# Down product of a decoder layer's feed-forward network: its weight blocks, from the fourth on, are requested on ScalarE's DMA queue instead of SyncE's

## The chip, the cores and the metric

The kernel runs on one core of one Trainium2 chip. The metric is the device time of one execution in microseconds (us), taken as the median of several runs. All tensors are float32. TensorE works on pairs: every operand is split into a high part of reduced precision (`fp32r`) and a low part (the rest), and each product is made of three matmuls (high x high, high x low, low x high).

## What is computed

One layer of a hybrid decoder on 1024 tokens of width 1024: feed-forward network 1, a token mixer (RWKV-7 and mLSTM side by side), attention over 256 memory tokens, feed-forward network 2, and a last RMSNorm. The change touches the two feed-forward networks alone:

```python
def _swiglu(h, w_gate, w_up, w_down):
    return (jax.nn.silu(h @ w_gate) * (h @ w_up)) @ w_down

x = x + 1/2 * SwiGLU_1(RMSNorm(x))      # D_MODEL = 1024, D_FF = 2816
...
x = x + 1/2 * SwiGLU_2(RMSNorm(x))
out = RMSNorm(x)
```

## The kernel before

There is no scheduler: each engine has its own instruction stream, written out by hand, and the streams meet at semaphores. Each engine works through its stream strictly in order, and so does each issuer of DMAs. SyncE (SP) issues nearly all loads. ScalarE (ACT) computes and issues a few DMAs of its own.

The function `ffn` exists once per engine and is called for network 1 and network 2. First come the gate and up products. Their result, the activation, has 22 tiles of 128 hidden channels x 1024 tokens, each with a high and a low part, 1 MB in all. Tiles 0 to 19 are stored to DRAM (`a_d`, L671), and the last two stay in SBUF (`act_new`). Then comes the down product, `G[n] += w_down[t].T @ a[t]`, and this is where the change is.

The down product runs in 2 x 22 blocks. The outer loop `h` takes the left and then the right half of the output channels (512 each), and the inner loop `j` takes the 22 hidden tiles in the order of the table `DOWN[h]`; `b = h * 22 + j` numbers the blocks 0 to 43. Block `b` needs

- its weights, 128 x 512 (256 KB), which travel through three steps: `load_down(b)` brings them from `in_wd` into one of three raw buffers `wd_raw[b % 3]` (named `sum_temp` in the trace); ACT rounds them to `v_hi` (`down_hi(b)`, L1630); POOL subtracts and makes `v_lo` (L923). `v_hi` and `v_lo` have four slots;
- its activation tile, brought by `load_tile` into `atile` (six places, L686) or `hhi`/`hlo` (L688, L689).

PE then makes 24 matmuls of 128 x 512 for the block (L1052 to L1054): 4 output groups x 2 halves of the tokens x 3. Of the last four blocks of each half (`TAIL`) the matmuls are ordered by output group, so that the results come out one after the other.

The waits around the change are these. `load_down(b)` waits until POOL has finished block `b - 3`, since the raw buffer is then free (semaphore `f_lo`). `down_hi(b)` waits for the landing of the weights (`f_wd`) and until PE has finished block `b - 4` (`f_prod`). PE waits for POOL's part of block `b` (`f_lo`) and for the tile (`f_load`).

Everything that SP loads for the down product stands in one stream (L703 to L744): weights 0 to 2 with tiles 0 to 5; tiles 6 to 9 (eight DMAs of 512 KB); weights 3; tiles 10 to 12 (six DMAs); four rows of x for the residual sum (`load_x`, L692, 512 KB each); weights 4, 5 and 6; tile 13; weights 7; tile 14; and so on, each later tile waiting until PE has left the place that it goes to. The two long runs of tiles and x in it are called bursts here.

Of the kernel before, what the change touches and what calls it, by code (L numbers as in the profile page):

```python
# [19 lines left out]
HALF = 512  # L20
# [3 lines left out]
FFC = FF // P  # L24
PAIRS = FFC // 2
BLOCKS = 2 * (PAIRS - 1)
TAIL = 4
DOWN = ((0, 1, 2, 3, 4, 5, 20, 21, 6, 7, 8, 9, 10, 11, 12, 13, 14, 15, 16, 17, 18, 19),
        (20, 21, 13, 14, 15, 16, 17, 18, 7, 8, 9, 10, 11, 12, 19, 6, 0, 1, 2, 3, 4, 5))
KIND = (0, 1, 3, 4, 2, 5, 6)  # L30
PLACE = tuple(KIND.index(n) for n in range(7))
WD_SLOTS, WD_RAWS = (3, 0, 1, 2), 3
# [26 lines left out]
ACT = mybir.ActivationFunctionType  # L59
# [36 lines left out]
def product_no(q, n):  # L96
    return 2 + 7 * q + n + 1


def down_no(h, j):  # L100
    return 2 + 7 * BLOCKS + h * (FFC - 1) + j + 1


def lo_no(q, n):
    return 4 + 7 * q + n + 1
# [6 lines left out]
def place_of(h, t):  # L112

    if t >= 20:
        return None
    if t == 19:
        return 6
    if t >= 13:
        return t - 13
    return 7 if h and t == 6 else t  # L120
# [55 lines left out]
def layer_kernel(nc, a, out):  # L176
# [3 lines left out]
    def sem(name):  # L180
        if name not in sems:
            sems[name] = ctx.enter_context(nc.semaphore(name))
        return sems[name]
# [74 lines left out]
    wd_raw = [s2_t, s1_t, s4_t]  # L258
# [121 lines left out]
    def weight_blocks(q):  # L380

        if q % 2 == 0:
            return [raw[:, r, s * HALF:(s + 1) * HALF] for r in range(2) for s in range(2)]
        return [xT[:, 2 * r + s, HALF:T] for r in range(2) for s in range(2)]

    def raw_at(f, q):

        return f_raw[q % 2].at(f, (q // 2 + (1 if q % 2 else 2)) * 32)

    def slot(hi, n):  # L390

        w, v = (whi, v_hi) if hi else (wlo, v_lo)
        return w[:, n // 2, n % 2 * HALF:(n % 2 + 1) * HALF] if n < 4 else v[:, n - 4, :]
# [33 lines left out]
    f_lo = Count2(sem("f_lo"), 4 + 7 * BLOCKS + 2 * FFC)  # L427
# [17 lines left out]
    f_wd = [Count2(sem(f"f_wd{n}"), (2 * FFC - n + WD_RAWS - 1) // WD_RAWS * 16) for n in range(WD_RAWS)]  # L445
# [136 lines left out]
    def _(sp):  # L582
# [72 lines left out]
        def ffn(f, after):  # L655

            wg, wu, wd = (a[f"{n}{f + 1}"] for n in ("wg", "wu", "wd"))
            x_from = x_park if f else a["x"]

            def load_pair(q):  # L660
                p = (q + 2) // 2
                for r in range(2):
                    if q % 2 == 0:
                        sp.dma_start(raw[:, r, :], wg[2 * p + r]).then_inc(f_raw[0].sem, 16)
                    else:
                        sp.dma_start(xT[:, 2 * r:2 * r + 2, HALF:T],
                                     wu[2 * p + r].rearrange("p (s c) -> p s c", s=2)).then_inc(f_raw[1].sem, 16)

            def store_pair(p):
                sp.wait_ge(*f_alo.at(f, 2 * p + 2))  # L670
                sp.dma_start(a_d[p], act_new[:].bitcast(F32)).then_inc(f_store.sem, 16)  # L671

            def load_down(b):
                h, j = divmod(b, FFC)
                if b < WD_RAWS:
                    sp.wait_ge(*f_lo.at(f, lo_no(BLOCKS - 1, PLACE[(1, 4, 6)[b]])))
                else:
                    sp.wait_ge(*f_lo.at(f, lo_no(BLOCKS, b - WD_RAWS)))
                sp.dma_start(wd_raw[b % WD_RAWS][:], wd[DOWN[h][j]][:, h * HALF:(h + 1) * HALF]).then_inc(
                    f_wd[b % WD_RAWS].sem, 16)  # L680

            def load_tile(h, t):
                at = place_of(h, t)
                src, s = a_d[t // 2][:, t % 2], f_load[at // 2].sem
                if at < 6:
                    sp.dma_start(atile[:, at].bitcast(F32), src).then_inc(s, 16)  # L686
                else:
                    sp.dma_start(hhi[:, at - 6, :].bitcast(F32), src[:, 0]).then_inc(s, 16)  # L688
                    sp.dma_start(hlo[:, at - 6, :].bitcast(F32), src[:, 1]).then_inc(s, 16)  # L689

            def load_x(k):
                sp.dma_start(xT[:, k, :], x_from[:, k, :]).then_inc(xc_in[k], 16)  # L692

            sp.wait_ge(split_made, after + credit)
            for r in range(2):
                sp.dma_start(raw[:, r, :], wu[r]).then_inc(f_raw[0].sem, 16)
            sp.wait_ge(*f_lo.at(f, 4))
            load_pair(0)
            sp.wait_ge(*f_tlo.at(f, 2))
            load_pair(1)  # L700
            for q in range(2, BLOCKS):
                sp.wait_ge(*f_lo.at(f, lo_no(q - 2, 5)))
                load_pair(q)  # L703
                if q % 2 == 0:
                    store_pair(q // 2 - 1)
            store_pair(PAIRS - 2)
            last = BLOCKS - 1
            load_down(0)
            sp.wait_ge(*f_store.at(f, (PAIRS - 1) * 16))
            for n, t in ((1, 0), (3, 2), (4, 4)):  # L710
                sp.wait_ge(*f_prod.at(f, product_no(last, PLACE[n])))
                load_tile(0, t)
                load_tile(0, t + 1)
                if t < 4:
                    load_down(t // 2 + 1)
            sp.wait_ge(*f_prod.at(f, product_no(last, 5)))
            for t in range(6, 10):
                load_tile(0, t)
            load_down(3)
            sp.wait_ge(*f_prod.at(f, product_no(last, 6)))  # L720
            for t in range(10, 13):
                load_tile(0, t)
            sp.wait_ge(*f_alo.at(f, 2 * PAIRS))
            for k in range(RC):
                load_x(k)
            for b in range(4, 2 * FFC):
                load_down(b)
                h, j = divmod(b - 6, FFC)
                if b < 6:
                    continue  # L730
                t = DOWN[h][j]
                if h == 0 and t < 7:
                    sp.wait_ge(*f_prod.at(f, down_no(0, j)))
                    load_tile(0, t + 13)
                if h == 1 and t == 21:
                    sp.wait_ge(*f_prod.at(f, down_no(1, j)))
                    for k in range(RC, KD):
                        load_x(k)
                if h == 1 and 13 <= t < 19:
                    sp.wait_ge(*f_prod.at(f, down_no(1, j)))  # L740
                    load_tile(1, t - 13)
                if h == 1 and t == 7:
                    sp.wait_ge(*f_prod.at(f, down_no(1, j)))
                    load_tile(1, 6)  # L744
# [786 lines left out]
    def _(act):  # L1531
# [68 lines left out]

        def ffn(f, gain, hi):

            silu = ACT.Silu

            def take_hi(q, n):

                a11, a12, a21, a22 = weight_blocks(q)
                kind = KIND[n]
                src = (a11, s2_t[:], a12, s3_t[:], s1_t[:], a22, s4_t[:])[kind]
                if kind in (0, 2, 5):  # L1610
                    act.wait_ge(*raw_at(f, q))
                else:
                    act.wait_ge(*f_sum.at(f, 4 * q + {1: 3, 3: 2, 4: 1, 6: 4}[kind]))
                if q:
                    act.wait_ge(*f_prod.at(f, product_no(q - 1, n)))
                elif n < 4:
                    act.wait_ge(unit_used, c.unit + 2 + credit)
                else:
                    act.wait_ge(*f_prod.at(f, 2 if n == 6 else 1))
                activation(slot(True, n), src, ACT.Copy).then_inc(f_hi.sem, 1)  # L1620

            def down_hi(b):
                act.wait_ge(*f_wd[b % WD_RAWS].at(f, (b // WD_RAWS + 1) * 16))
                if b >= 4:
                    act.wait_ge(*down_free(f, b - 4))
                elif b:
                    act.wait_ge(*f_prod.at(f, product_no(BLOCKS - 1, b + 3)))
                else:
                    act.wait_ge(*f_prod.at(f, 2))
                activation(v_hi[:, WD_SLOTS[b % 4], :], wd_raw[b % WD_RAWS][:], ACT.Copy).then_inc(f_hi.sem, 1)  # L1630
# [55 lines left out]
            def chunk_hi(k):  # L1686
                if gain:
                    activation(hi[:, k, :], xT[:, k, :], ACT.Copy, scale=v1(gain, k)).then_inc(*nh_act.sig(f"c{k % 2}"))

            for b in range(3, 2 * FFC):  # L1690
                down_hi(b)
                if b == FFC - 1:
                    square(0)
                    square(1)
                if b == FFC + 1:
                    square(2)
                if b == FFC + 3:
                    square(3)
# [1015 lines left out]
```

## Time and profile before

| | |
|---|---|
| time, median of 3 runs | 2914.01 us (2911.01 to 2915.51) |
| the profiled execution's own time | 2909.36 us |
| its span, first to last instruction | 2907.6 us |
| granted TensorE clock, mean over the span | 0.979 of full |
| PE busy | 2755.8 us (95%) |
| ACT busy | 814.3 us (28%) |
| POOL busy | 1513.3 us (52%) |
| DVE busy | 1349.6 us (46%) |
| moved by DMA | 383.06 MB, mean 132 GB/s |
| down products, first and last PE instruction | about 455 to 700 us, and 2623 to 2870 us of the span |

"Busy" counts compute instructions. An instruction that issues a DMA is listed under the engine's queue (SPq, ACTq) and has its own duration. The DMA queue of SP is q1 in the profile, that of ACT is q10. The chain of waits is followed back from the last instruction; what stands in it is what set the end.

### The profile page before, as it was taken

To read this page: it belongs to the slowest core of one execution; us is meant where nothing else is said; L and a number is where in the kernel's file an instruction comes from. 1 tells how busy PE (TensorE), PEld (TensorE's weight loads), DVE (VectorE), ACT (ScalarE), POOL (GpSimd) and SP (SyncE) were. 2 spreads that over 40 slices of the span, in tenths; PEclk is the share of its full clock that TensorE was granted. 3 is DMA by queue.
4 is the path that set the end of the run, shared out by engine and by line. 5 is a ranking of instruction groups with operands and counts; after the bars stand their busy time and mean duration, and the time that the engine had idled before them with its cause. 6 is when DMAs were issued, how large, how long until landed. Compare 5 with 4: busy or idle time off the path is not lost.

```text
span 2907.6 us, 35919 instructions
## 1 busy us (share of the span) xinstructions
PE 2755.8 (95%) x14214; PEld 2278.1 (78%) x14214; DVE 1349.6 (46%) x1357; ACT 814.3 (28%) x1203; POOL 1513.3 (52%) x899
## 2 busy tenths in 40 slices
PE   6999998999999999998999999998899999998996
PEld 5888887888788877777777778888787888887885
DVE  8444441014456535776777645443346444440203
ACT  4333331112001113443444332213413333331111
POOL 4988882123794623555555434431036988872220
PEclk9999999999999999998999999999999999999998
DMA  3333228252862654344334264113021332338151
GB/s 118 117 116 116 108 99 347 69 202 79 342 222 90 217 192 134 99 106 139 105 103 102 70 226 154 44 58 130 0 87 67 121 113 105 116 120 327 59 181 65
DMA packets 143171, 383.06 MB, mean 132 GB/s; under 512 B 10156, under 2 KB 61612, under 8 KB 128832
## 3 DMA queue, kind: packets, MB, share of 16 engines
q1 hardware_dynamic: 119936, 317.75, 31.7%
q10 hardware_dynamic: 23104, 63.47, 5.8%
q8 instruction: 94, 1.54, 0.2%
q14 instruction: 37, 0.30, 0.0%
HBM read 272.57 MB, written 108.58 MB: 131 GB/s over the span
## 4 chain that ended last, share of the span: by engine, by line
PE 73%; issue 9%; POOL 6%; DVE 5%; DMA 2%; ACT 1%; SPq 1%; ACTq 1%; POOLq 0%; DVEq 0%
PE G L1052 14%; PE G L1054 14%; PE G L1053 14%; PE G L977 8%; PE G L979 8%; PE G L978 8%; PE G L1190 2%; POOL AL L868 2%; PE G L1475 1%; DMA sum_temp<-in_wd 1%; PE G L1227 1%; DMA zrw_d<-po 1%; DVE nt_b L2051 1%; POOL Tr L862 1%; ACTq L1546 0%
## 5 line engine op out<-in xcount | busy, mean ns | idle before, releaser
L939 POOL TENSOR_TENSOR whi<-raw,zero 128x1024 fp32r<-128x1024 f32 x67 | 130.2, 1943 | 472.7 <-PE G L979 387.7
L923 POOL TENSOR_TENSOR v_lo<-sum_temp,v_hi 128x512 fp32r<-128x512 f32 x88 | 117.2, 1335 | 383.6 <-ACT v_hi L1630 383.6
L1052 PE MATMUL G<-hhi,v_hi 128*128 128x512 f32 x800 | 312.0, 390 | 0.0
L1054 PE MATMUL G<-hhi,v_lo 128*128 128x512 f32 x800 | 311.2, 389 | 0.0
L1053 PE MATMUL G<-hlo,v_hi 128*128 128x512 f32 x800 | 311.2, 389 | 0.0
L977 PE MATMUL G<-hhi,whi 128*128 128x512 f32 x688 | 272.3, 396 | 28.8 <-POOL wlo L942 21.9
L978 PE MATMUL G<-hlo,whi 128*128 128x512 f32 x688 | 270.8, 394 | 0.0
L979 PE MATMUL G<-hhi,wlo 128*128 128x512 f32 x688 | 270.3, 393 | 0.0
L1190 PE MATMUL G<-hq,gw 128*128 128x512 f32 x768 | 223.7, 424 | 9.8 <-DVE ev L2330 4.6
L1052 PE MATMUL G<-t_hi,whi 128*128 128x512 f32 x480 | 186.7, 389 | 0.0
L1053 PE MATMUL G<-t_lo,whi 128*128 128x512 f32 x480 | 186.7, 389 | 0.0
L1054 PE MATMUL G<-t_hi,wlo 128*128 128x512 f32 x480 | 186.7, 389 | 0.0
L942 POOL TENSOR_TENSOR wlo<-raw,whi 128x1024 fp32r<-128x1024 f32 x67 | 176.3, 2631 | 5.3
L1190 PEld LDWEIGHTS G<-hq,gw 128*128 128x128 f32 x768 | 139.3, 194 | 48.3 <-issue 20.3
L977 PEld LDWEIGHTS G<-hhi,whi 128*128 128x128 f32 x688 | 130.9, 190 | 58.3 <-POOL wlo L942 22.7
L2237 DVE SCALAR_TENSOR_TENSOR rtmp<-G,nrx 128x1024 f32<-128x1024 f32 x16 | 19.6, 1223 | 335.5 <-PE G L1054 335.4
L1053 PEld LDWEIGHTS G<-hlo,v_hi 128*128 128x128 f32 x800 | 150.2, 188 | 31.7 <-issue 0.5
L1052 PEld LDWEIGHTS G<-hhi,v_hi 128*128 128x128 f32 x800 | 150.2, 188 | 31.5 <-issue 0.5
L1054 PEld LDWEIGHTS G<-hhi,v_lo 128*128 128x128 f32 x800 | 150.2, 188 | 31.2
L1052 PE MATMUL G<-atile,v_hi 128*128 128x512 f32 x384 | 153.8, 400 | 18.2 <-POOL v_lo L923 18.2
L1630 ACT ACTIVATE v_hi<-sum_temp 128x512 fp32r<-128x512 f32 x88 | 55.7, 633 | 399.5 <-PE G L1054 309.2
L919 POOL TENSOR_TENSOR wlo<-sum_temp,whi 128x512 fp32r<-128x512 f32 x120 | 165.3, 1399 | 3.4 <-ACT whi L1620 3.4
(409 smaller groups left out, 6378.9 us busy)
## 6 DMA issues: line engine op xcount, KB each, us to landing
a_d<-act_new SPq DMA_DIRECT2D x20, 2048.0 KB, 6.3
atile<-a_d SPq DMA_DIRECT2D x36, 1024.0 KB, 7.1
gw<-gw_d SPq DMA_DIRECT2D x32, 1024.0 KB, 5.4
raw<-in_wg SPq DMA_DIRECT2D x44, 512.0 KB, 4.0
sum_temp<-in_wd SPq DMA_DIRECT2D x88, 256.0 KB, 3.4
xT<-in_wu SPq DMA_DIRECT2D x40, 512.0 KB, 4.6
gw_d<-gw SPq DMA_DIRECT2D x16, 1024.0 KB, 4.8
hhi<-a_d SPq DMA_DIRECT2D x18, 512.0 KB, 13.2
```

The costliest lines, as they stand in the source:

```text
L868: tt(AL[:, n % 2], Am[:], copies(C_LEV + n * P), ALU.mult).then_inc(*F.sig(f"am{n}"))
L919: tt(slot(False, n), src, slot(True, n).bitcast(F32), ALU.subtract).then_inc(f_lo.sem, 1)
L923: tt(v_lo[:, k, :], wd_raw[b % WD_RAWS][:], v_hi[:, k, :].bitcast(F32), ALU.subtract).then_inc(f_lo.sem, 1)
L939: nc.gpsimd.tensor_tensor(whi[:, k, 0:w], raw[:, k, 0:w], zero[:].to_broadcast([P, w]), ALU.add).then_inc(hi_made, 1)
L942: nc.gpsimd.tensor_tensor(wlo[:, k, 0:w], raw[:, k, 0:w], whi[:, k, 0:w].bitcast(F32), ALU.subtract).then_inc(split_made, 1)
L977: nc.tensor.matmul(dst, wh, hi, start=start, stop=False)
L978: nc.tensor.matmul(dst, wh, lo, start=False, stop=False)
L979: return nc.tensor.matmul(dst, wl, hi, start=False, stop=stop)
L1052: nc.tensor.matmul(dst, wh, hi, start=start, stop=False, skip_group_check=True)
L1053: nc.tensor.matmul(dst, wh, lo, start=False, stop=False, skip_group_check=True)
L1054: return nc.tensor.matmul(dst, wl, hi, start=False, stop=stop, skip_group_check=True)
L1190: last = nc.tensor.matmul(G[3][:, 1, :], gw[:, k, way == 2, t * P:(t + 1) * P], hq[:, t + (way == 1) * KD, :], start=at == 0, stop=at == 3 ...
```

## The change

The weights of blocks 0 to 2 are still issued by SP. Those of blocks 3 to 43 are issued by ACT: 3 and 4 after ACT's last work on the activation, and `load_down(b + 2)` ahead of `down_hi(b)` from then on, so 5 ahead of 3, 6 ahead of 4. The condition of each issue is the same semaphore at the same value as before. It is ACT that waits for it now. On SP the same calls are gone, and the tile and x loads keep their order and their own waits.

```diff
@@ sync: ffn @@
             def load_down(b):
                 h, j = divmod(b, FFC)
-                if b < WD_RAWS:
-                    sp.wait_ge(*f_lo.at(f, lo_no(BLOCKS - 1, PLACE[(1, 4, 6)[b]])))
-                else:
-                    sp.wait_ge(*f_lo.at(f, lo_no(BLOCKS, b - WD_RAWS)))
+                sp.wait_ge(*f_lo.at(f, lo_no(BLOCKS - 1, PLACE[(1, 4, 6)[b]])))
...
             for t in range(6, 10):
                 load_tile(0, t)
-            load_down(3)
             sp.wait_ge(*f_prod.at(f, product_no(last, 6)))
             for t in range(10, 13):
                 load_tile(0, t)
             sp.wait_ge(*f_alo.at(f, 2 * PAIRS))
             for k in range(RC):
                 load_x(k)
-            for b in range(4, 2 * FFC):
-                load_down(b)
+            for b in range(6, 2 * FFC):
                 h, j = divmod(b - 6, FFC)
-                if b < 6:
-                    continue
@@ scalar: ffn @@
+            def load_down(b):
+                h, j = divmod(b, FFC)
+                act.wait_ge(*f_lo.at(f, lo_no(BLOCKS, b - WD_RAWS)))
+                act.dma_start(wd_raw[b % WD_RAWS][:], wd[DOWN[h][j]][:, h * HALF:(h + 1) * HALF]).then_inc(
+                    f_wd[b % WD_RAWS].sem, 16)
...
+            load_down(3)
+            load_down(4)
             for b in range(3, 2 * FFC):
+                if b + 2 < 2 * FFC:
+                    load_down(b + 2)
                 down_hi(b)
```

The order on SP at the end of the second burst, network 1, before (`hhi`, `hlo` and `atile` are activation tiles, `sum_temp` the weights' raw buffers, `xT` the rows of x):

```order
L688 DMA hhi<-a_d 128x1024
L689 DMA hlo<-a_d 128x1024
L679 DMA sum_temp_72<-in_wd 128x512 [waits f_lo]
L688 DMA hhi<-a_d 128x1024 [waits f_prod]
...
L692 DMA xT<-in_x 128x1024 [waits f_alo]
L692 DMA xT<-in_x 128x1024 x3
L679 DMA sum_temp_71<-in_wd 128x512 [waits f_lo]
L679 DMA sum_temp_74<-in_wd 128x512 [waits f_lo]
L679 DMA sum_temp_72<-in_wd 128x512 [waits f_lo]
L686 DMA atile<-a_d 128x2048 [waits f_prod]
L679 DMA sum_temp_71<-in_wd 128x512 [waits f_lo]
L686 DMA atile<-a_d 128x2048 [waits f_prod]
```

and the same place now:

```order
L686 DMA hlo<-a_d 128x1024
L685 DMA hhi<-a_d 128x1024 [waits f_prod]
...
L689 DMA xT<-in_x 128x1024 [waits f_alo]
L689 DMA xT<-in_x 128x1024 x3
L683 DMA atile<-a_d 128x2048 [waits f_prod] x6
```

The weights that stood between tile 9 and tile 10, and behind the x rows, have left SP.

The order on ACT at the start of the down product, network 1, before (`v_hi` are the rounded weights, `act_new` the last two activation tiles):

```order
L1630 ACTIVATE v_hi<-sum_temp_74 128x512 [waits f_prod,f_wd2]
L1644 ACTIVATE act_new<-gs 128x1024 [waits f_gs,f_store]
L1644 ACTIVATE act_new<-gs 128x1024 [waits f_gs]
L1630 ACTIVATE v_hi<-sum_temp_72 128x512 [waits f_prod,f_wd0]
L1630 ACTIVATE v_hi<-sum_temp_71 128x512 [waits f_prod,f_wd1]
```

and now:

```order
L1629 ACTIVATE v_hi<-sum_temp_74 128x512 [waits f_prod,f_wd2]
L1643 ACTIVATE act_new<-gs 128x1024 [waits f_gs,f_store]
L1643 ACTIVATE act_new<-gs 128x1024 [waits f_gs]
L1618 DMA sum_temp_72<-in_wd 128x512 [waits f_lo]
L1618 DMA sum_temp_71<-in_wd 128x512 [waits f_lo]
L1618 DMA sum_temp_74<-in_wd 128x512 [waits f_lo]
L1629 ACTIVATE v_hi<-sum_temp_72 128x512 [waits f_prod,f_wd0]
L1618 DMA sum_temp_72<-in_wd 128x512 [waits f_lo]
L1629 ACTIVATE v_hi<-sum_temp_71 128x512 [waits f_prod,f_wd1]
```

Three weight requests stand together ahead of the rounding of block 3, and then one stands ahead of each rounding, with its own wait for POOL.

## Rows read from the trace of the kernel before

**Rows 1.** The page: the chain of waits, shares of the span by line.

```profile
PE G L1052 14%; PE G L1054 14%; PE G L1053 14%; PE G L977 8%; PE G L979 8%; PE G L978 8%; PE G L1190 2%; POOL AL L868 2%; PE G L1475 1%; DMA sum_temp<-in_wd 1%; PE G L1227 1%; DMA zrw_d<-po 1%; DVE nt_b L2051 1%; POOL Tr L862 1%; ACTq L1546 0%
```

**Rows 2.** The chain in order of time: start us, us, what.

```profile
471.71 14.53 DMA sum_temp<-in_wd
486.98 1.27 POOL v_lo L923
...
2640.32 14.81 DMA sum_temp<-in_wd
```

**Rows 3.** Timeline of PE, network 1, around blocks 3 and 4: start, duration, instruction.

```profile
471.12 0.39 PE L1054 MATMUL G<-atile,v_lo 128*128 128x512 f32 x1
474.83 0.50 PE L1052 MATMUL G<-atile,v_hi 128*128 128x512 f32 x1 [3.32 <-POOL v_lo L923]
...
488.29 0.79 PE L1052 MATMUL G<-atile,v_hi 128*128 128x512 f32 x1 [6.12 <-POOL v_lo L923]
...
495.74 0.39 PE L1052 MATMUL G<-atile,v_hi 128*128 128x512 f32 x1
```

**Rows 4.** The same in network 2.

```profile
2639.49 0.39 PE L1054 MATMUL G<-atile,v_lo 128*128 128x512 f32 x1
2643.71 0.80 PE L1052 MATMUL G<-atile,v_hi 128*128 128x512 f32 x1 [3.83 <-POOL v_lo L923]
...
2657.18 0.80 PE L1052 MATMUL G<-atile,v_hi 128*128 128x512 f32 x1 [4.97 <-POOL v_lo L923]
...
2665.56 0.39 PE L1052 MATMUL G<-atile,v_hi 128*128 128x512 f32 x1
```

**Rows 5.** PE by stretch: us, PE busy (count), granted clock, DMA share, GB/s.

```profile
2643.00:2649.00 6.00, 5.29 (x13) 0.50 1.02 408
```

**Rows 6.** Timeline of SP's queue, network 1, second burst.

```profile
456.54 2.25 SPq L679 DMA_DIRECT2D sum_temp<-in_wd  x1
...
466.60 5.07 SPq L692 DMA_DIRECT2D xT<-in_x  x4
471.71 3.42 SPq L679 DMA_DIRECT2D sum_temp<-in_wd  x3
```

**Rows 7.** Timeline of ACT in both networks; in brackets its idle time and the releaser.

```profile
457.45 2.00 ACT L1644 ACTIVATE act_new<-gs 128x1024 fp32r<-128x1024 f32 x2
...
486.27 1.96 ACT L1630 ACTIVATE v_hi<-sum_temp 128x512 fp32r<-128x512 f32 x3 [12.83 <-DMA sum_temp<-in_wd]
...
501.44 0.63 ACT L1630 ACTIVATE v_hi<-sum_temp 128x512 fp32r<-128x512 f32 x1 [4.81 <-PE G L1054]
...
2626.30 1.99 ACT L1644 ACTIVATE act_new<-gs 128x1024 fp32r<-128x1024 f32 x2
```

**Rows 8.** DMAs issued at 456.5, 773 and 753 us: KB, us to landing; q1 at 773.

```profile
sum_temp<-in_wd SPq DMA_DIRECT2D x1, 256.0 KB, 16.2
...
q1 hardware_dynamic: 55, 0.41, 107.0%
...
zrw_d<-po ACTq DMA_DIRECT2D x1, 512.0 KB, 6.8
...
graw<-in_gates_in SPq DMA_DIRECT2D x1, 512.0 KB, 13.4
```

**Rows 9.** DMA queues from 735 to 738 us: packets, MB, share of 16 engines.

```profile
q1 hardware_dynamic: 220, 0.78, 64.2%
q10 hardware_dynamic: 219, 0.45, 38.8%
```

**Rows 10.** ACT's DMA issues by line: duration ns min/median/max, first and last start.

```profile
L1712 ACTq DMA_DIRECT2D zrw_d<-po x14: 337/338/1019, 749.7 to 880.7; - x14
L1546 ACTq DMA_DIRECT2D h_d<-hlo x2: 609/5090/9570, 723.7 to 727.9; - x2
```

**Rows 11.** Timeline of ACT between the halves of the product, network 1.

```profile
584.40 0.63 ACT L1630 ACTIVATE v_hi<-sum_temp 128x512 fp32r<-128x512 f32 x1 [2.90 <-PE G L1054]
...
593.92 0.63 ACT L1630 ACTIVATE v_hi<-sum_temp 128x512 fp32r<-128x512 f32 x1 [1.26 <-PE G L1054]
```

More of the change, by code:

```diff
@@ L1601, in ffn @@
         def ffn(f, gain, hi):
-            silu = ACT.Silu
+            silu, wd = ACT.Silu, a[f"wd{f + 1}"]
             def take_hi(q, n):
```

## The prediction, made before the changed kernel ran

> **What bounds the kernel now.** I read the page first. The chain of waits is mostly PE's lines, but one line in it is not work: the transfer of the down weights, `sum_temp<-in_wd`, has 1% of the span [rows 1]. The chain in order of time says where: two pieces, one in each network, of 14.5 and 14.8 us, each followed by POOL's `v_lo` of 1.27 us [rows 2]. So twice in the run a 256 KB load is what everything waits for.
>
> PE's timeline at these places shows what it costs. In network 1 PE starts the last matmul of block 2 at 471.12, stands 3.32 us before block 3 and 6.12 us before block 4, and starts block 5 at 495.74 [rows 3]. In network 2 it stands 3.83 and 4.97 us [rows 4]. Behind each pause the granted clock is 0.50, the lower of the two levels (1.2 GHz), for some us [rows 5], so a pause costs more than its length.
>
> The reason for the late weights is on SP's queue. Weights 3 are issued at 456.54 behind eight tile DMAs; weights 4, 5 and 6 at 471.71, only after six more tile DMAs and the four x rows [rows 6]. The DMA engines are full in these stretches (share 1.02, about 410 GB/s [rows 5]), so a request lands when all that stands ahead of it on its queue has gone through: weights 3 took 16.2 us [rows 8]. ACT stood 12.83 us for weights 4 [rows 7], and POOL and PE behind it.
>
> **What the pauses are worth.** In steady state ACT's rounding comes every 4.81 + 0.63 = 5.44 us, released by PE [rows 7]; that is one block of 24 matmuls, 0.2267 us each. From the last matmul of block 2 to the first of block 5 there are 49 starts, 11.11 us at that pace. Network 1 took 495.74 - 471.12 = 24.62 us, so it loses 13.51. Network 2 took 2665.56 - 2639.49 = 26.07 us and loses 14.96. The sum is **28.5 us**. The pauses are 18.2 of it, and the lower clock behind the four pauses is the other 10.2, so 2.6 us for a pause.
>
> **Part 1: weights 3, 4 and 5 leave SP's queue.** ACT is free for its first request when the last `act_new` is done, at 457.45 + 2.00 = 459.45 in network 1 and at 2628.29 in network 2 [rows 7]. It is 3 us later than SP's old request for weights 3, and 12 us earlier than for weights 4. The semaphore for weights 3 and 4 (blocks 0 and 1 done by POOL) has long been reached. When do they land? No load of before was issued by ACT with SP's backlog ahead of it at this depth. The nearest row is ACT's store at 773 us: 512 KB, issued while q1 had the engines (share 1.07), landed after 6.8 us [rows 8]. The other end is the mirror case, SP's load of 512 KB at 753 us, across ACT's backlog and behind two loads of its own queue: 13.4 us [rows 8]. Sooner than 6.8 changes nothing. I take 6.8, since it is the same queue against the same backlog, and my load has half the bytes.
>
> The two queues share the engines packet by packet: from 735 to 738 us, with both full, they had 220 and 219 packets [rows 9]. The bytes differ since the packets do; q10 got 0.45 of 1.23 MB there with the small ones, some 150 GB/s, so each further weight of 0.26 MB lands about 1.8 us after the one before.
>
> From the start of rounding to PE is 2.0 us (486.27 to 488.29 [rows 7, 3]). Network 1: 459.45 + 6.8 + 2.0 = 468.3, and PE wants block 3 at 471.12 + 0.23 = 471.35, so 3.0 us to spare. Network 2: 2628.29 + 6.8 + 2.0 = 2637.1 against 2639.72, so 2.6 us to spare. Weights 4 land at about 468.1 and weights 5 at 469.9; PE wants them at 476.8 and 482.2. All four pauses go: **-28.5 us**. With 13.4 in place of 6.8 block 3 is late by 3.5 and 4.0 us in the two networks; with 2.6 of lower clock each this gives back 12.7, and 15.8 remain.
>
> The Trainium skill, *DMA: Bandwidth & Descriptors*, section "Issuing engines are not separate DMA queues", speaks against the change: DMAs of all issuers end on the same 16 engines, and issuing from several engines only saves the sequencer's time. Taken alone it would leave the weights behind the backlog; the rival below has that in numbers. The packet counts of rows 9 do not agree with it for the latency of one request. The same page, under "Arbitration", has each DMA engine alternate between its queues, which is what the rows show.
>
> **Part 2: SP without the weights.** SP's stream is shorter by 41 requests in each network. Tiles and x keep their conditions. Their queue carries the same bytes minus 0.77 MB in the burst, which now go on the other queue. What is late next? Tiles 6 to 12, issued by 466.6, are first wanted in block 8, some 27 us after block 3 starts; tile 13, issued at 475.1 behind the x rows and weights 4 to 6 [rows 6], in block 15. At the 16.2 us of a full queue they land by 483 and 492, against 498 and 537. Nothing: 0 us.
>
> **Part 3: ACT's new waits.** Each rounding now stands behind a request, and each request behind POOL's finish of block b - 1. In steady state: rounding 0.63, handover and POOL 1.4, request 0.34 [rows 2, 7, 10], 2.4 us in a period of 5.44. The wait for PE ends last, as before. Price 0, as long as a request takes below 3.0 us. While three requests stand together (459.5 to about 461) nothing behind them is ready to round.
>
> Between the halves ACT also squares finished rows, and the request for block 24 waits behind two of these. At 584.40 it rounds block 22, and PE has finished that block at 593.9 [rows 11]. Now block 23 is rounded after POOL's block 22, at about 586.8, and is ready at 588.8, 5.1 us before PE wants it at 593.9. Price 0.
>
> **Sum.** Profiled execution: 2909.4 - 28.5 = 2880.9 us. The median of the runs shown is 4.65 us above the profiled one, so I take the median: 2914.0 - 28.5 = **2885.5 us**, 1.0% faster. What follows each product (norm, stores, next product) waits for its result, so the first network's gain is handed on.
>
> **Rivals.**
> 1. *Weights land late but alone* (the 13.4 us end): pauses before block 3 stay, those before block 4 go. 2914.0 - 15.8 = 2898.2. For it: requests across a full queue did take 7 to 13 us. Against: the slow ones were on the other queue and larger.
> 2. *No overtaking*: ACT's requests wait out SP's backlog, 16.2 us as weights 3 did. Ready at 477.7 and 2646.5, 6.3 and 6.8 us late, plus 5.2 of lower clock: 28.5 - 18.3 = 10.2 gained, 2903.8. This is the rule quoted above. Against it: rows 9, and the 6.8 us of rows 8.
> 3. *No change*: the burst is bound by bytes, the weights take their share from the tiles, and PE waits for tiles instead. 2914. Against it: the 15 us and more to spare in part 2.
> 4. *Slower*: ACT is held in its own requests. One request of ACT took 9.57 us at 727.9 us [rows 10]. If each did so as long as the burst fills the engines, from 459.5 until the tile issued at 475.1 has landed 16.2 us later, 32 us, a block would take 9.57 + 2.1 = 11.7 in place of 5.44: 2.7 blocks instead of 5.9, 17 us lost in each network, and three pauses more in each with 2.6 us of lower clock: 2914.0 - 28.5 + 34 + 15.6 = 2935. It decides from 3.3 us a request. Against it: that row is the last of four large stores in a row on ACT's own queue, which here holds three weights of 256 KB; the 14 stores of 512 KB took 0.34 us in the median and 1.02 at most.
>
> **How the numbers follow.** Forecast 0.78; rival 1 0.08; rival 2 0.06; rival 3 0.04; rival 4 0.04. About 0.2% (6 us) is what a measurement can tell from no change. The first three cases are faster by more: 0.92; same 0.04; slower 0.04. The range goes from 2885.5 less the runs' own spread of 4.5 us, 2881, to rival 1 with 1 us more, 2899; rivals 2 to 4, 0.14 together, lie outside.
>
> **What would show it.** In the changed profile the pauses of PE before blocks 3 and 4 are gone and the granted clock stays at 1.00 there; `sum_temp<-in_wd` is gone from the chain; the weights on ACTq land in some 7 us in the bursts; ACT's requests last 0.34 us; the rounding of block 3 starts at about 466 us and that of block 4 waits for POOL. If PE still stands before block 3, rivals 1 or 2 hold, by the landing time; if it stands before tiles, rival 3; if requests on ACTq exceed 3 us, rival 4.

## The result, and the profile after

| | before | after |
|---|---|---|
| median | 2913.34 us (4 runs) | 2883.69 us (4 runs, 2876.65 to 2883.99) |
| ratio to before, 95% interval | | 0.9894 [0.9879, 0.9909] |
| the profiled execution's own time | 2909.36 us | 2876.65 us |
| its span | 2907.6 us | 2874.9 us |
| granted clock, mean | 0.979 | 0.986 |

The time fell by 1.06%, 30 us, where 28.5 us were forecast. The changed kernel ran twice more as a control, with ratios of 0.9890 [0.9870, 0.9911] and 0.9893 [0.9878, 0.9909].

The chain of waits by line, on the page of the changed kernel, has no weight transfer any more (before: [rows 1]):

```profile
PE G L1045 15%; PE G L1047 15%; PE G L1046 15%; PE G L970 8%; PE G L971 8%; PE G L972 8%; POOL AL L861 2%; PE G L1183 2%; PE G L1468 1%; DMA zrw_d<-po 1%; PE G L1220 1%; POOL Tr L855 1%; DVE nt_b L2054 1%; ACTq L1539 0%; ACT sx L1969 0%
```

PE by stretch (length, busy time and count, granted clock, DMA share, GB/s), where it stood before [rows 3 to 5]; first network 1, then network 2:

```profile
471.00:475.00 4.00, 4.00 (x19) 1.00 1.03 401
...
482.00:488.00 6.00, 6.00 (x28) 1.00 1.03 406
...
2600.00:2660.00 60.00, 60.00 (x266) 1.00 1.02 407
```

PE is busy all the time at full clock, while the DMA engines are as full as before. The bytes are the same, only their order on the engines is not.

ACT's timeline in network 1, the counterpart of [rows 7]:

```profile
456.91 0.86 ACTq L1618 DMA_DIRECT2D sum_temp<-in_wd  x2
457.33 2.00 ACT L1643 ACTIVATE act_new<-gs 128x1024 fp32r<-128x1024 f32 x2
458.83 0.33 ACTq L1618 DMA_DIRECT2D sum_temp<-in_wd  x1
463.88 0.63 ACT L1629 ACTIVATE v_hi<-sum_temp 128x512 fp32r<-128x512 f32 x1 [4.55 <-DMA sum_temp<-in_wd]
...
466.63 0.63 ACT L1629 ACTIVATE v_hi<-sum_temp 128x512 fp32r<-128x512 f32 x1 [2.12 <-PE G L1047]
...
469.10 0.63 ACT L1629 ACTIVATE v_hi<-sum_temp 128x512 fp32r<-128x512 f32 x1 [1.83 <-POOL v_lo L916]
```

Block 3 is rounded at 463.88, 7.0 us after the request, and PE goes over to it only at about 471; block 4 is rounded at 466.63 instead of 486.27. The DMA queues from 463 to 466 us show how the weights got past the backlog (packets, MB, share of 16 engines):

```profile
q1 hardware_dynamic: 228, 0.82, 68.0%
q10 hardware_dynamic: 223, 0.42, 36.3%
```

Both queues moved nearly the same number of packets, as in [rows 9]: the engines take from each in turn. The requests of the burst (KB, median us to landing), SP's tiles issued from 472.5 to 488.2 us first:

```profile
atile<-a_d SPq DMA_DIRECT2D x6, 1024.0 KB, 20.8
```

and ACT's two requests at 456.91:

```profile
sum_temp<-in_wd ACTq DMA_DIRECT2D x2, 256.0 KB, 7.7
```

The two weights take 7.7 us in the median, the first of them, weights 3, 6.9 us, instead of 16.2 [rows 8]. What they gain, the tiles pay. A tile requested at 456.43 us lands after

```profile
hhi<-a_d SPq DMA_DIRECT2D x1, 512.0 KB, 20.4
```

where one requested at 456.04 us took 16.1 us before. The 20.8 us above are no measure of that: five of the six tiles were requested only at 488.64 us and later before, behind weights on the same queue. The first of the six is landed at 493.5 us now (472.69 + 20.8) and was at 490.1 before (475.17 + 14.9), so tiles come 3 to 4 us later. They have that time to spare.

**Where the time went.** Four events, the same in both kernels, mark the ends of three stretches. The first rounding of the down weights starts at 441.30 before and 441.20 after in network 1, at 2609.68 and 2592.16 in network 2; the second of the last four outputs of network 1's down product is taken over by DVE at 701.95 and 688.34; the last step of the program starts at 2894.11 and 2861.42:

```profile
701.95 1.22 DVE L2237 SCALAR_TENSOR_TENSOR rtmp<-G,nrx 128x1024 f32<-128x1024 f32 x1
```

before, and after:

```profile
688.34 1.23 DVE L2240 SCALAR_TENSOR_TENSOR rtmp<-G,nrx 128x1024 f32<-128x1024 f32 x1
```

So the down product of network 1 is 13.5 us shorter (13.61 less the 0.10 at its start), what lies between the networks' products 3.9 us, and the rest with network 2's product 15.2 us. The forecast had 13.51 and 14.96 for the two products. The two control profiles of the changed kernel repeat the products to 0.2 us: 247.14 and 247.13 us in network 1 (247.14 here, 260.65 before), 269.22 and 269.37 from the second event to the end (269.26 here, 284.43 before). The stretch between the products does not repeat: it is 1907.7 us before, and 1903.8, 1912.1 and 1910.8 us in the three profiles of the changed kernel. So its 3.9 us can't be put down to the change.

One part of them can be seen. In the profile of before, a spell of lower clock lies at 1698 us, at the end of the token mixer, and the changed kernel's profile has none there. PE by stretch before, and the same place after, 16 us earlier in the program's time:

```profile
1698.00:1705.00 7.00, 6.46 (x18) 0.56 0.94 360
```

```profile
1682.00:1689.00 7.00, 4.21 (x18) 1.00 1.00 385
```

By DVE's steps, the changed kernel is 14.1 us ahead in front of this place (`Bm<-cst,G` at 1617.59 and 1603.47) and 15.8 us behind it (`mo<-sg,G` at 1717.57 and 1701.81). So 1.6 us go with the spell. Another 1.7 us come near 2015 us (`mx<-G` at 2018.93 and 2001.41), where the clock was 0.83 before (2010 to 2020 us) and 1.00 after (1994 to 2004 us).

Such spells come and go between executions of one kernel: the control run has one at 1645 us (`1645.00:1655.00`: clock 0.52) that neither of these two has, and by DVE's steps it is 4.2 us behind the first profile in front of it (`Bm<-cst,G` at 1607.67 against 1603.47) and over 8 us behind at its end. Its span is 2884.1 us, not 2874.9.

### The profile page after: what moved, and what is told of

Same layout as the page of the kernel before. It is cut to its first block, busy times and chain, and to the rows that moved or that the text cites. A ratio compares the mean times of both kernels' runs of the same rounds, so it can differ in the third digit from the quotient of the medians.

```text
span 2874.9 us, 35919 instructions
## 1 busy us (share of the span) xinstructions
PE 2739.7 (95%) x14214; PEld 2267.4 (79%) x14214; DVE 1349.6 (47%) x1357; ACT 812.7 (28%) x1203; POOL 1512.2 (53%) x899
## 4 chain that ended last, share of the span: by engine, by line
PE 74%; issue 10%; POOL 7%; DVE 4%; DMA 2%; ACT 1%; ACTq 1%; SPq 0%; POOLq 0%; DVEq 0%
PE G L1045 15%; PE G L1047 15%; PE G L1046 15%; PE G L970 8%; PE G L971 8%; PE G L972 8%; POOL AL L861 2%; PE G L1183 2%; PE G L1468 1%; DMA zrw_d<-po 1%; PE G L1220 1%; POOL Tr L855 1%; DVE nt_b L2054 1%; ACTq L1539 0%; ACT sx L1969 0%
## 5 line engine op out<-in xcount | busy, mean ns | idle before, releaser
L972 PEld LDWEIGHTS G<-hhi,wlo 128*128 128x128 f32 x688 | 131.0, 190 | 27.8
## 6 DMA issues: line engine op xcount, KB each, us to landing
hhi<-a_d SPq DMA_DIRECT2D x18, 512.0 KB, 15.2
```

What stands on the lines that cost most here:

```text
L972: return nc.tensor.matmul(dst, wl, hi, start=False, stop=stop)
```

## The experiments

Two things were to be told apart. Why were the weights late: because of what stood ahead of them on their own queue (my theory), or because the DMA engines were full? And what is a pause of PE worth: is each a cost of its own, or does PE wait only for the latest of what it needs? Eleven further runs follow; ratios are to the kernel before, run on the same chip. "Longer" and "shorter" of a product are by the events above, against the 247.14 and 269.26 us of the changed kernel.

**The control (again).**

> The changed kernel once more, as the control of this study. Both theories: 2884 us, ratio 0.989 to 0.991 to the kernel before. PE has no pause of over 0.5 us in the two down products. The one profiled execution of the change was 7 us faster than its other three runs and lacked a 6.8 us spell of lower clock that the kernel before had at 1698 us of its span; if such a spell is there in this profile, the time is near 2884, if not, near 2877.

2882.9 us (2876.85 to 2885.88), ratio 0.9890 [0.9870, 0.9911]. No pause of PE in either product. The spell at 1698 us is missing and there is one at 1645 us. So I had the place wrong; that a profile with such a spell comes near 2884 us (2885.88) came out.

**Only three requests on the second queue (only345).** SP's `load_down` waits as in the kernel before.

```diff
 # sync
             for b in range(6, 2 * FFC):
+                load_down(b)
                 h, j = divmod(b - 6, FFC)
 # scalar
             load_down(3)
             load_down(4)
+            load_down(5)
             for b in range(3, 2 * FFC):
-                if b + 2 < 2 * FFC:
-                    load_down(b + 2)
                 down_hi(b)
```

> Only weights 3, 4 and 5 go over ScalarE's queue, weights 6 to 43 are back on SyncE's. Theory (three requests overtake one burst): nearly the whole gain, 2884 to 2890 us. Weights 6 are issued behind the x rows at about 472 us, land some 14.5 us later and are ready at about 488.3, PE wants them at 487.7: a pause of 0 to 2 us before block 6 in each network. Rival (the gain needs all weights off SyncE, since its queue is in arrears for the whole product): 2895 us or more, with pauses before several blocks.

2889.9 us, ratio 0.9917 [0.9899, 0.9935]. PE's waits in the two products are one each, 2.0 and 2.2 us, before block 6 (waits in total, times, longest; network 1):

```profile
PE G L1049 <- POOL v_lo L920: 2.0, 1, 2.0
```

ACT's timeline:

```profile
464.57 0.63 ACT L1633 ACTIVATE v_hi<-sum_temp 128x512 fp32r<-128x512 f32 x1 [3.95 <-DMA sum_temp<-in_wd]
466.54 0.63 ACT L1633 ACTIVATE v_hi<-sum_temp 128x512 fp32r<-128x512 f32 x1 [1.33 <-DMA sum_temp<-in_wd]
468.47 0.63 ACT L1633 ACTIVATE v_hi<-sum_temp 128x512 fp32r<-128x512 f32 x1 [1.31 <-DMA sum_temp<-in_wd]
489.09 0.63 ACT L1633 ACTIVATE v_hi<-sum_temp 128x512 fp32r<-128x512 f32 x1 [19.98 <-DMA sum_temp<-in_wd]
```

Blocks 3, 4 and 5 came over ACT's queue 1.95 us apart (1.8 forecast from the shares of rows 9); weights 6, back behind the x rows on SP's, at 489.09. The rival, pauses before several blocks and 2895 us or more, is out. Three requests per network bring some three quarters of the gain. The other 38 matter by one: the first that is back behind the burst.

**The same queue, another order (sp_order).**

```diff
 # sync, in the kernel before
             sp.wait_ge(*f_prod.at(f, product_no(last, 5)))
+            load_down(3)
             for t in range(6, 10):
                 load_tile(0, t)
-            load_down(3)
+            load_down(4)
...
             for t in range(10, 13):
                 load_tile(0, t)
+            load_down(5)
...
             for b in range(4, 2 * FFC):
-                load_down(b)
+                if b > 5:
+                    load_down(b)
```

> No second queue: the kernel before, with the weights' requests further forward in SyncE's own stream (3 ahead of tiles 6 to 9, 4 behind them, 5 ahead of the x rows). Theory (what counts is how many bytes stand ahead on the same queue): weights 3 and 4 are in time (4: issued at about 456.5, lands about 472.7, ready 474.8, wanted 476.8), weights 5 are late by 1.5 us in network 1 and 2.5 in network 2. 2890 to 2895 us. Rival (only a second queue helps): 2914 us.

2890.6 us, ratio 0.9926 [0.9905, 0.9947]. PE's waits are 1.8 and 1.9 us, before block 5, and the products are 2.4 and 2.8 us longer. Weights 4 were rounded at 474.06, where 474.8 less 2.0 was forecast. A few lines of order on one queue do what the second queue does, up to one late block.

**The same queue, the x rows out of the burst (one_queue).**

```diff
 # sync, in the kernel before
-            load_down(3)
             sp.wait_ge(*f_prod.at(f, product_no(last, 6)))
+            load_down(4)
+            load_down(5)
             for t in range(10, 13):
                 load_tile(0, t)
-            sp.wait_ge(*f_alo.at(f, 2 * PAIRS))
-            for k in range(RC):
-                load_x(k)
-            for b in range(4, 2 * FFC):
+            for b in range(6, 2 * FFC):
                 load_down(b)
                 h, j = divmod(b - 6, FFC)
-                if b < 6:
-                    continue
+                if b == 14:
+                    sp.wait_ge(*f_alo.at(f, 2 * PAIRS))
+                    for k in range(RC):
+                        load_x(k)
```

(with `load_down(3)` ahead of tiles 6 to 9, as in the run above)

> No second queue: weights all on SyncE, 3 ahead of tiles 6 to 9, 4 and 5 ahead of tiles 10 to 12, and the four x rows only ahead of tile load of block 14 (they are wanted at the end of the first half). Theory (a load is late by the bytes that stand ahead of it on its own queue, nothing else): weights 4 and 5 land at about 474 to 475, weights 6 at about 483 against 487.7 wanted: no pause in either network, 2883 us, as the changed kernel. Rival (the second queue gives something that no order on one queue gives): 2890 us or more.

2885.4 us (2876.8 to 2888.17), ratio 0.9900 [0.9886, 0.9915]; the changed kernel beside it on the same chip 2882.7 us, 0.9893 [0.9878, 0.9909]. The intervals overlap. PE has no wait in either product, and the products take 247.13 and 269.37 us, to 0.1 us what the changed kernel takes. ACT's timeline:

```profile
463.18 0.63 ACT L1631 ACTIVATE v_hi<-sum_temp 128x512 fp32r<-128x512 f32 x1 [3.15 <-DMA sum_temp<-in_wd]
474.11 1.29 ACT L1631 ACTIVATE v_hi<-sum_temp 128x512 fp32r<-128x512 f32 x2 [10.30 <-DMA sum_temp<-in_wd]
483.47 0.63 ACT L1631 ACTIVATE v_hi<-sum_temp 128x512 fp32r<-128x512 f32 x1 [8.07 <-DMA sum_temp<-in_wd]
```

Weights 4 and 5 at 474.11 and weights 6 at 483.47, as forecast (474 to 475, 483). The second queue gave nothing here that an order on one queue doesn't give.

**A second backlog on ACT's own queue (x_on_act).**

```diff
 # sync
-            sp.wait_ge(*f_alo.at(f, 2 * PAIRS))
-            for k in range(RC):
-                load_x(k)
 # scalar
+            act.wait_ge(*f_alo.at(f, 2 * PAIRS))
+            for k in range(RC):
+                act.dma_start(xT[:, k, :], (x_park if f else a["x"])[:, k, :]).then_inc(xc_in[k], 16)
             load_down(3)
             load_down(4)
```

> The change, but the four x rows (2 MB) go over ScalarE's queue too, ahead of weights 3. Theory (a queue is in order within itself, and two queues share the engines packet by packet): issued at about 462, 2 MB at half of 410 GB/s is 10 us, weights 3 land at about 478 and are ready at 480, PE stands 9 us before block 3 in each network: about 2908 us. Rival (ScalarE's queue is served ahead of SyncE's): the 2 MB take 5 us, pause 4 us, about 2898 us. Rival (requests on ScalarE's queue are fast whatever is ahead of them): 2884 us.

2906.8 us (10 runs, 2899.36 to 2912.79), ratio 0.9977 [0.9964, 0.9989]. PE stood 8.2 and 8.9 us before block 3. The requests of weights 3 to 5 stand behind 2 MB on their own queue (issued 463 to 465 us; weights 3 are rounded 14.7 us after their request, against 7.0 us in the changed kernel):

```profile
462.93 1.74 ACTq L1615 DMA_DIRECT2D sum_temp<-in_wd  x3
477.61 0.63 ACT L1626 ACTIVATE v_hi<-sum_temp 128x512 fp32r<-128x512 f32 x1 [18.40 <-DMA sum_temp<-in_wd]
```

and from 467 to 475 us the two queues moved the same number of packets, now with packets of the same size:

```profile
q1 hardware_dynamic: 454, 1.66, 51.9%
q10 hardware_dynamic: 454, 1.60, 50.3%
```

Weights were rounded at 477.61 where "landed at about 478" was forecast. This is the run that rules most out. Requests on ACT's queue are not fast whatever stands ahead of them (2884 us by that rival), nor is the queue served first (a pause of 4 us and 2898 us by that one): in the changed kernel it was merely empty.

**A later request (late).**

```diff
 # scalar
+            act.wait_ge(*f_prod.at(f, down_no(0, 1)))
             load_down(3)
             load_down(4)
```

> The change, but ScalarE waits until PE has finished block 1 before it requests weights 3, 4 and 5 (PE reaches that at about 465.9 us, against 457 without the wait). Theory (the requests overtake, and what they need is some 7 us from request to landing under the burst): weights 3 land at about 472.8, ready at 474.8, PE stands 3.5 us before block 3 in each network and loses 2.6 us more to the lower clock: 2883 + 12 = 2895 us. Rival (the gain comes from the order on the queues alone, the moment of the request counts for nothing): 2883 us.

2891.9 us, ratio 0.9935 [0.9919, 0.9952]. PE:

```profile
475.59 0.50 PE L1045 MATMUL G<-atile,v_hi 128*128 128x512 f32 x1 [3.22 <-POOL v_lo L916]
...
2634.50 0.80 PE L1045 MATMUL G<-atile,v_hi 128*128 128x512 f32 x1 [3.16 <-POOL v_lo L916]
```

Requested at 466.96, rounded at 473.56, 6.6 us later. So the latency under the burst is 6.6 to 7.0 us in these two runs, at two places in the burst. The products are 5.1 and 5.2 us longer for 3.2 us of standing each; the difference of 1.9 us goes with a lower clock behind the pause (0.84 from 474 to 485 us). Against the ratio of the control (0.9890) the run lost 0.0045 of 2911, 13 us, with an uncertainty of some 8 us from the two ratios; the 10.3 us of the profile are the better number.

**One part of the change alone, and the other (only3, all_but3).**

```diff
 # only3: sync as before without load_down(3); scalar
+            load_down(3)
             for b in range(3, 2 * FFC):
                 down_hi(b)
```

> Only weights 3 go over ScalarE's queue; 4 and all later ones stay behind the x rows on SyncE's. Theory (PE waits for the latest of what it needs, pauses do not add): no pause before block 3, one of about 9 us before block 4 in each network in place of 3.3 + 6.1. What is saved is the lower clock behind one of two pauses, 0 to 2.6 us in each network: 2908 to 2913 us. Rival (each pause is a cost of its own, as my sum of four terms has it): the pause before block 3 is saved, 12.7 us, 2901 us.

2911.4 us (10 runs), ratio 1.000 [0.9991, 1.001]. PE stands once in each network, 11.4 and 11.9 us, before block 4:

```profile
488.80 0.80 PE L1051 MATMUL G<-atile,v_hi 128*128 128x512 f32 x1 [11.41 <-POOL v_lo L922]
```

It starts block 4 at 488.80, before it was 488.29 [rows 3]. The pause before block 3 is gone, all of it is stood off before block 4. The products take 261.0 and 284.3 us, where the kernel before took 260.7 and 284.4. I had 9 us for the pause: the sum of the old pauses. But block 3, which ran partly at the lower clock before, is now faster too, and that time is waited for as well.

```diff
 # all_but3: scalar as in the change without load_down(3); sync
             for t in range(6, 10):
                 load_tile(0, t)
+            load_down(3)
```

> Weights 3 stay on SyncE's queue between tile 9 and tile 10, weights 4 to 43 go over ScalarE's. Theory: the pause before block 3 stays at 3.5 to 5.5 us in each network (weights 3 now share the engines with 4 and 5), with 2.6 us of lower clock each; the one before block 4 goes. 2883 + 12 to 16 = 2895 to 2899 us. Together with the kernel that moves weights 3 alone the two parts give less than the whole.

2896.9 us, ratio 0.9949 [0.9933, 0.9966]. PE stands 4.2 and 5.2 us before block 3. Weights 3, still on SP's queue and requested at 457.58 us, landed after 17.1 us (16.2 before), ACT's weights 4, requested at 457.72 us, after 6.7:

```profile
sum_temp<-in_wd SPq DMA_DIRECT2D x1, 256.0 KB, 17.1
sum_temp<-in_wd ACTq DMA_DIRECT2D x1, 256.0 KB, 6.7
```

That pair is the cleanest measurement of the mechanism: the same source, size and moment, two queues. One part brings 0.0%, the other 0.5%, both together 1.1%. The parts don't add, as forecast.

**The same rule at another place (rest_later, after_5, rest_5).** The chain of waits of the changed kernel still has `zrw_d<-po`: the first stores of the projections behind network 1, which stand behind 8 MB of parked tokens, the norm and the constants on ACT's own queue.

```diff
 # scalar
         norm_root(nms_a[:], nrm[:])
         park_tokens()                    # now without the norm
-        act.dma_start(cst[:, C_HONES:NCONST], a["consts"][:, C_HONES:NCONST]).then_inc(consts_in, 16)
         project_rw()
+        park_rest()                      # the norm, and the constants
```

(`park_rest` is new: it holds the two requests, which stood ahead of `project_rw`.)

> The change, and the same rule applied elsewhere: behind network 1, ScalarE's queue holds 8 MB of parked tokens, then the norm (0.5 MB) and constants (1.3 MB), and only then the first store of the projections (zrw_d), which is in the chain of waits with 22 us. Here norm and constants are issued after these stores. Theory (what stands ahead on the same queue delays a transfer): that store lands 5 to 9 us sooner and PE loses 3 to 8 us less near 745 to 765 us: 2876 to 2881 us. Rival (PE waits there for SyncE's loads, which share the engines anyway): 2883 us.

2878.1 us, ratio 0.9886 [0.9870, 0.9903]. The pause near 761 us was gone, but the interval of this run and those of the changed kernel, which ran on other chips, left open whether the time was.

> The changed kernel a third time, beside the next two on one chip. Both theories: 0.9895 of the kernel before, within 0.002.

> The change with the norm and the constants issued behind the projections' stores, again. Theory: PE's pause of 4 to 5 us near 761 us is gone and that stretch is 5 to 6 us shorter, as in the first profile of this kernel, so 5 to 6 us below the changed kernel of this same call: ratio 0.987 to 0.988. Rival (given back later, since the constants come later): equal to the changed kernel.

Side by side on one chip: the changed kernel 2882.7 us (2879.33 to 2885.16), ratio 0.9893 [0.9878, 0.9909]; with norm and constants later **2875.3 us** (2872.68 to 2879.33), ratio 0.9871 [0.9856, 0.9886], the lowest median of all. The two intervals still overlap, from 0.9878 to 0.9886. PE's waits from 700 to 1040 us in the changed kernel:

```profile
PE G L970 <- DVEq L2280: 4.8, 1, 4.8
PE G L970 <- POOL wlo L935: 3.3, 1, 3.3
```

and in the one with the stores first:

```profile
PE G L970 <- POOL wlo L935: 3.3, 1, 3.3
```

The wait that is gone is PE's for DVE, which waits for the landing of the first stores, since it writes to their buffers next. ACT's queue with the changed kernel, and with the stores first:

```profile
723.29 7.96 ACTq L1541 DMA_DIRECT2D h_d<-nrm  x1
731.28 3.44 ACTq L1992 DMA_DIRECT2D cst<-in_consts  x1
735.05 2.33 ACTq L1715 DMA_DIRECT2D zrw_d<-po  x2
```

```profile
724.70 9.59 ACTq L1718 DMA_DIRECT2D zrw_d<-po  x2
```

The two stores take as long to land after their request as they did, 23.0 and 23.1 us in the median. What moved is the request: ACT starts on the first at 724.70 instead of 735.05 us, since those of norm and constants (7.96 and 3.44 us, blocked in issue) are no longer ahead. The stores land at 750.8 and 751.8 us instead of 757.7 and 760.1, so 7 and 8 us sooner, within the 5 to 9 us forecast.

The profiles settle what the overlapping intervals leave open. This one runs 1.15 us behind that of the changed kernel in front of the stores (the norm on ACT at 709.70 and 708.55 us) and 6.5 us ahead from 768 us on (`stg<-G,nrm` at 768.14 and 774.64), so 7.6 us are gained there, 4.8 of them the pause. They are not given back when the constants are wanted: it is 6.5 us ahead at 1070 us too (`ev<-G,hq` at 1069.56 and 1076.02). The rival is out, and the gain, 7.4 us in the medians, is more than the 5 to 6 us forecast.

## Why the prediction was right

It was right, by the steps it gave:

- *What the pauses are worth, 28.5 us.* The two products got shorter by 13.5 and 15.2 us in the profiles (13.51 and 14.96 forecast). The measured 30 us, and 31 and 32 us by the two controls' ratios, are a little more; 28.5 us is a ratio of 0.990, inside all three intervals. In the three profiles of the changed kernel the products give 28.7, 28.7 and 28.6 us. Whether the excess of 1 to 3 us is real stays open; it does not come from the products.
- *ACT is free for its first request at 459.45.* Wrong by 2.5 us, on the safe side: the requests went out at 456.91, while ACT was still rounding block 2 and had `act_new` ahead of it in the program.
- *Landing after 6.8 us.* Weights 3 landed after 6.9 us, the two requested together after 7.7 in the median; the first was rounded 7.0 us after its request. Weights 4 were forecast to land at 468.1 us and were being rounded at 466.63. The nearest row was the right one to take, though it was a store of twice the size; the other end, 13.4 us, never came up.
- *SP without the weights: nothing is late next.* Right. But I took 16.2 us for the landing of tiles, and with the weights on the other queue they took up to 20.4 us in the first burst. The queue that gives way gets half of the packets as long as the other has some. The margin of 15 us and more was enough.
- *ACT's new waits: 0.* Right: 82 requests at 0.33 us in the median, 0.45 the longest, and in steady state the rounding is again released by PE after 4.81 us. Between the halves, block 23 was rounded 2.7 us behind block 22 (2.4 forecast). The prediction gives the longest request without harm once as 3.0 and once as 3.3 us; its own terms give 5.44 - 0.63 - 1.4 = 3.4. At 0.33 us nothing hangs on it.
- *One sign failed.* The rounding of block 4 was to wait for POOL. It waited for PE (2.12 us, at 466.63); the one of block 5 waited for POOL (1.83 us, at 469.10). The requests went out earlier than forecast, so this costs nothing.
- *Rival 2 and the rule behind it.* The Trainium skill, *DMA: Bandwidth & Descriptors*, section "Issuing engines are not separate DMA queues", says that issuing from several engines saves only the sequencer's time, which is usually small beside the DMA's own. It does not say that a request waits for another queue's backlog; that was my reading. For a single small request behind a backlog the runs disagree with the advice: 6.7 against 17.1 us at one moment. For the throughput of the whole they agree: 406 GB/s in 19 us of network 2's burst before (2620 to 2639 us) and 404 after (2603 to 2622 us). What the same page says under "Arbitration", that each engine alternates between queues packet by packet, is what x_on_act shows, 454 to 454 packets.
- The price of a single pause, 2.6 us of lower clock and its own length, was used in the rivals as if pauses were independent. The run with weights 3 alone shows that they aren't: it saves nothing. The sum does not depend on that, since it takes the stretch from block 2 to block 5 as a whole, and all the late loads go at once.

## What to carry to other kernels

A load that PE needs soon, issued behind a burst that nobody needs soon, waits for every byte of the burst: look at the landing time of the small request beside the bytes issued ahead of it on the same queue. Either take it to a queue that is empty at that moment, or ask for it ahead of the burst, or put part of the burst later. Here the first (0.9893) and the last two together (0.9900) were worth the same, and the last two need no second engine; asking ahead alone left one block late (0.9926). Before changing, count when the next load would be late too: pauses of an engine that waits for several late loads don't add, so moving one of them may bring nothing.

## What the runs showed of the hardware

- Two DMA queues that both have work move the same number of packets: 228 and 223 with packets of different sizes (0.82 and 0.42 MB), 454 and 454 with equal ones (1.66 and 1.60 MB). The queue with the small packets got a third of the bytes.
- A request of 256 KB on an empty queue took 6.3 to 6.9 us to land while the other queue was full (the first requests in only345, late, all_but3 and the changed kernel). In the quiet of 520 to 660 us of the changed kernel it took 2.4 us at least and 3.3 in the median. Each further one behind it came 1.95 us later, so I estimate the transfer itself at less than a third of the time under load.
- An issue blocks when much stands ahead on its own queue: 7.96 and 3.44 us for two requests behind 8 MB of stores, against 0.33 us for a request of weights. What stands behind it on that engine's queue waits too.
- An engine's DMA requests went out ahead of compute instructions that stand before them in its program but were still queued: two weights' requests from 456.91 us, `act_new` from 457.33.
- The clock of PE behind a pause: after 3.2 us of standing in late it was 0.50, the lower level, from 477 to 480 us, and the pause cost 5.1 us in all. After 1.8 and 1.9 us in sp_order it stayed at 1.00 (490 to 500 and 2650 to 2662 us). Spells of lower clock in the token mixer (around 1645 and 1698 us) differ between executions of the same kernel and move its time by several us.
